# The order of the query blocks in a head pair's attention: 0 to 7, or small and large in turn

## What is computed

```python
SEQ, N_HEADS, HEAD_DIM, N_KV_HEADS = 1024, 8, 64, 2      # 4 query heads per KV head
CMP_BLOCK, CMP_STRIDE, SLC_BLOCK, TOP_K, WINDOW, Q_BLOCK = 32, 16, 64, 16, 512, 128

def nsa_core(q, qpos, gates, cmp_kv, fetch, n_sel, win_kv, win_pos):
    ...
    s = jnp.einsum('btkgd,bnkd->bkgtn', qg, cmp_kv[:, :, 0]) - slopes * d_c.astype(F32)
    p_cmp = masked_softmax(s, d_c >= 0)
    o_cmp = jnp.einsum('bkgtn,bnkd->btkgd', p_cmp, cmp_kv[:, :, 1])
    ...
    _, idx = lax.top_k(score, min(TOP_K, n_sel))
    sel = fetch(idx)
    ...
    p = masked_softmax(s, d_s >= 0)
    o_slc = jnp.einsum('bkgtm,bktmd->bkgtd', p, vsel)
    ...
    mask_w = (d_w >= 0) & (d_w < WINDOW) & (win_pos[None, :] >= 0)
    p = masked_softmax(s, mask_w)
    o_win = jnp.einsum('bkgts,bskd->btkgd', p, win_kv[:, :, 1].astype(F32))
    o = g[:, :, 0] * o_cmp + g[:, :, 1] * o_slc + g[:, :, 2] * o_win
```

## Time and profile before

| | us |
|---|---|
| median of 3 runs | 1961.72 (1958.79 to 1964.0) |
| the profiled execution | 1964.53 |
| its span | 1962.7 |
| mean granted TensorE clock | 0.974 |

### The profile page before, as it was taken

One profiled execution on the slowest core, in us unless ns is written; L12 is line 12 of the kernel. 1 busy time (PEld: TensorE's weight loads), 2 busy tenths in 40 slices (PEclk: granted clock), 3 DMA queues, 4 the chain that ended last, 5 costly groups with the idle time before them and its releaser, 6 DMA issues.

```text
span 1962.7 us, 35065 instructions
## 1 busy us (share of the span) xinstructions
PE 1869.0 (95%) x13394; PEld 1744.7 (89%) x13394; DVE 913.8 (47%) x1621; ACT 658.5 (34%) x1229; POOL 599.1 (31%) x611
## 2 busy tenths in 40 slices
PE   7999989998996989999999999999999999999998
PEld 6999979988994666666799999999999999999898
DVE  5699945665446666767533221212121212224434
ACT  4312222344334666566522321211111121214335
POOL 0003872322304433334353222222222222225531
PEclk8999987999998999999999999999999999999998
DMA  5322364533513344333313112111111111112113
GB/s 156 90 77 52 76 184 112 158 91 101 159 45 108 101 122 125 116 118 114 111 54 127 43 33 59 33 55 38 49 39 53 43 44 54 38 44 92 54 33 132
DMA packets 192571, 163.66 MB, mean 83 GB/s; under 512 B 23092, under 2 KB 175361, under 8 KB 191759
## 3 DMA queue, kind: packets, MB, share of 16 engines
q1 hardware_dynamic: 174781, 137.01, 23.7%
q0 software_dynamic: 6336, 17.31, 3.3%
q10 hardware_dynamic: 11290, 7.09, 1.3%
HBM read 147.70 MB, written 18.25 MB: 85 GB/s over the span
## 4 chain that ended last, share of the span: by engine, by line
PE 32%; issue 23%; POOL 8%; DVE 3%; ACT 2%; POOLq 0%; DVEq 0%; ACTq 0%
PE ps L206 10%; POOL wm_lo L192 6%; PE ps L2168 5%; PE ps L2540 4%; PE ps L1610 3%; PE ps L1622 3%; PE ps L1599 3%; PE ps L1649 2%; DVE S L1868 1%; PE ps L2557 1%; ACT S L1749 1%; PE ps L1657 1%; PE ps L1685 1%; POOL S L1566 1%; PE ps L2577 0%
## 5 line engine op out<-in xcount | busy, mean ns | idle before, releaser
L192 POOL TENSOR_TENSOR wm_lo<-wm_raw,wm_hi 128x512 fp32r<-128x512 f32 (+1 forms) x96 | 169.1, 1762 | 556.8 <-ACT wm_hi L187 556.8
L2357 DVE TENSOR_TENSOR xT<-ps,xT 128x1056 f32<-128x1056 f32 x64 | 80.5, 1258 | 259.9 <-PE ps L206 259.9
L1566 POOL TENSOR_SCALAR S<-S,inv,gate_p 128x64 f32<-128x64 f32 (+6 forms) x192 | 123.2, 662 | 207.2 <-DVE inv L1878 207.2
L206 PE MATMUL ps<-Ahi,wm_hi 128*128 128x352 f32 x768 | 167.5, 326 | 4.4 <-POOL wm_lo L192 2.5
L187 ACT ACTIVATE wm_hi<-wm_raw 128x512 fp32r<-128x512 f32 (+1 forms) x96 | 73.9, 769 | 286.4 <-PE ps L206 286.4
L206 PE MATMUL ps<-Hhi,wm_hi 128*128 128x352 f32 x768 | 167.1, 326 | 1.3 <-POOL wm_lo L192 1.3
L902 PE MATMUL ps_p<-Xhi,w1hi 128*128 128x256 f32 (+1 forms) x544 | 164.4, 302 | 2.9 <-DVE Xlo L1087 2.9
L206 PE MATMUL ps<-Alo,wm_hi 128*128 128x352 f32 x768 | 166.0, 324 | 0.0
L206 PE MATMUL ps<-Ahi,wm_lo 128*128 128x352 f32 x768 | 166.0, 323 | 0.0
L206 PE MATMUL ps<-Hhi,wm_lo 128*128 128x352 f32 x768 | 165.6, 323 | 0.0
L206 PE MATMUL ps<-Hlo,wm_hi 128*128 128x352 f32 x768 | 165.3, 323 | 0.0
(11 more groups left out here) (383 smaller groups left out, 3999.0 us busy)
## 6 DMA issues: line engine op xcount, KB each, us to landing
s_raw<-in_cache_slc_kv_dram SPq DMA_DIRECT2D x256, 128.0 KB, 2.1
raw<-in_cache_cmp_kv_dram SPq DMA_DIRECT2D x128, 128.0 KB, 4.2
raw<-in_cache_cmp_kv_dram POOLq DMA_DIRECT2D x128, 128.0 KB, 4.4
wm_raw<-in_w_up_dram SPq DMA_DIRECT2D x32, 512.0 KB, 4.0
wm_raw<-in_w_down_dram SPq DMA_DIRECT2D x64, 256.0 KB, 2.7
win_raw<-in_w_in_dram SPq DMA_DIRECT2D x38, 256.0 KB, 3.4
wg_raw<-in_w_ple_gate_dram SPq DMA_DIRECT2D x14, 512.0 KB, 3.9
xT<-x_spill SPq DMA_DIRECT2D x2, 2112.0 KB, 10.8
```

What stands on the lines that cost most here:

```text
L192: self.c.nc.gpsimd.tensor_tensor(self.lo[s][:, 0:nk, :], self.raw[s % self.raw_slots][:, 0:nk, :], self.hi[s][:, 0:nk, :].bitcast(F32), AL ...
L206: mm = nc.tensor.matmul(ps[:, j, 0:CH], w[s][:, k, :], x(k)[:, CH * j:CH * j + CH], start=(k == 0 and n == 0), stop=(k == nk - 1 and n == 2))
L1566: nc.gpsimd.tensor_scalar(x, x, inv[:, n % 3, 3 * e + br:3 * e + br + 1], c.gate_p[:, i, H * br + h:H * br + h + 1], ALU.mult, ALU.mult).t ...
L2357: nc.vector.tensor_tensor(three(x), banks[s][:, :, 0:CH], three(x), ALU.add).then_inc(W.free, 1)
```

## The change

Two tables are changed. The blocks of a head pair are taken in the order 0, 7, 1, 6, 2, 5, 3, 4, and the tiles of scores have other places, such that three neighbours of the new order don't overlap. What follows from the order changes with it: the units scored ahead of the first step are blocks 0 and 7; block 0 hosts 1, block 7 hosts 6, 1 hosts 2, 6 hosts 5, 2 hosts 3, 5 hosts 4, 3 hosts the next pair's 0, and 4 its 7; the last units are blocks 3 and 4.

```diff
-S_PLACE = {7: 0, 6: 6912, 5: 13312, 4: 0, 3: 5376, 1: 9728, 0: 13312, 2: 14592}
+BLOCK_ORDER = (0, 7, 1, 6, 2, 5, 3, 4)
+S_PLACE = {7: 0, 6: 6912, 5: 13312, 4: 7680, 3: 3328, 1: 14336, 0: 13056, 2: 0}
...
-    UNITS = [(g, i) for g in range(G) for i in range(QB)]
+    UNITS = [(g, i) for g in range(G) for i in BLOCK_ORDER]
```

## The result

The changed kernel takes 1972.87 us in the median of 5 runs (1970.81 to 1974.06), against 1961.72 (1958.79 to 1964.0): a ratio of 1.0054, 95% interval 1.0044 to 1.0065. It is slower, by 11 us. 1976 was forecast.

The account below looks back on a forecast made before the run. The attention stage was taken to last TensorE's own work plus its idle time. Terms 10.2 + 2.3 - 2.9 + 2.65 + 1.5 = 13.75 us over 1961.7 gave 1976 us; own range 1969 to 1984, 8 in 10 within 1960 to 1988.

Parts of the forecast that it names:

- part 1: Block 0 before block 7, three places: 6.26 us chain against 2.88 us of TensorE work; idle 8.9 us in sum.
- part 3: Decoding quads' exps on ScalarE: TensorE's waits for them grow from 5.9 to 8.2 us, +2.3 us.
- part 4: ScalarE's copy of finished output blocks: TensorE's waits for it fall from 10.3 to 7.4 us, -2.9 us.
- smaller waits: TensorE's other idle time, with the end of the stage some 9 us; no change entered in the sum.
- part 5: Start of the attention stage, blocks 0 and 7 scored ahead: +4.5 us, less 1.85 of work already done, +2.65 us.
- part 6: TensorE's clock falls behind two of the three long waits, the old fall gone or moved: +1.5 us, bounds 0 and 3.
- Part 2: Blocks 1, 2 and 3 before 6, 5 and 4: waits for scaled scores of 3.3, 2.6 and 0.6 us.
- three long waits: TensorE's waits of part 1: 3.4 us at steps 44 and 66, 2.1 us at step 22.
- rival (a): No difference within 0.3%: the waits don't add up and the constants hide the start; 5 us, 1967; chance 0.19.
- Rival (b): Faster: large blocks' light steps are filled, 17 us won against 12.9 of new waits and start; 1957; chance 0.15.
- Rival (c): Slower by more: the clock falls after every wait over 1.2 us, some ten times, +15 us; 1989; chance 0.08.

Follow-up runs that it names:

- e1: The changed kernel again, unedited: 1975.72 us, ratio 1.0061.
- e2: The changed kernel, with ScalarE doing block 7's late exps before keeping the transposed bank in block 0's one step: 1967.33 us, ratio 1.0023.
- e5: The old order, with ScalarE copying the finished output before keeping the transposed bank in step 1 of a unit: 1954.29 us, ratio 0.9951.
- e4: The changed kernel, with the first head pair in the old order and score tiles placed unit by unit: 1972.16 us, ratio 1.0057.
- e7: The changed kernel with the ScalarE list edits of e2, e5 and e6: 1951.73 us, ratio 0.9938.
- e6: The old order with e5's edit, and ScalarE doing a quad's exps before the late exps of the hosted block: 1950.60 us, ratio 0.9939.
- e3: The changed kernel, with 24 extra TensorE transposes in the wait before block 7 in the third and fourth pair: 1970.17 us, ratio 1.0046.

## Why the prediction was right, point by point

The time is 3 us under the forecast in the first measurement and at the forecast in e1 (1975.72); the sign and the places of the long waits are right. That the sum comes out to 0.1 us for the stage is luck: the clock was put 7.4 us too low, and the other terms together as much too high, the waits for scaled scores alone by 3.1.

| term of the sum | predicted us | in the profile after |
|---|---|---|
| part 1, block 0 before 7 (in the next row too) | 8.9 | 3.35 + 3.35 + 2.1 = 8.8 |
| parts 1 and 2, all waits for scaled scores | 15.4 (+10.2) | 10.4, and 12.3 with the 1.9 us for VectorE's queue (+7.1) |
| part 3, quads' exps | 8.2 (+2.3) | 8.2 (+2.3) |
| part 4, output copy | 7.4 (-2.9) | 5.9 (-4.4) |
| smaller waits | 0 | -1.9, without the 1.9 counted above |
| part 5, start, net of work done ahead | +2.65 | 4.04 - 2.35 = +1.7 |
| part 6, clock | +1.5 | 331.8 - (325.2 - 2.35) = +8.9 |
| the stage | +13.75 | +13.7 |

- Part 1 holds to 0.1 us, link by link: the step above is the chain that was worked out. In the second pair the last link was another one than named. VectorE's queue behind the blocked reciprocal held the bank for the quad's scores, and TensorE waited 1.9 us for that and 0.2 for GpSimd. The prediction has that queue in it, but said that it lies inside the same 6.3 us, which it does. e2 shows that the place of the late exps is the cause of 1.4 of the 3.35 us in the third pair and of 2.2 in the fourth.
- Part 2 was too high. Block 1 before 6 gave 1.6, 0, 1.1 and 0.1 us for 1.7, 0, 1.3 and 0.3, but block 2 before 5 gave 0, 0, 0.4 and 0.4 for 2.6 in all, and block 3 before 4 nothing for 0.6. There other waits of the same step (a kept bank of keys 0.6, the quads' exps) came first and covered it. That is rival (a)'s mechanism at work in the small.
- Part 3's sum is right, and so are its places: quads 1, 4, 5, 6, 11 and 13. The single waits are off by up to 0.2 us.
- Part 4's sign and cause hold; its size was under-estimated by 1.5 us. e5 says how to read it: most of the old order's waits were due to the copy's place behind the keep.
- Part 5: the first transposes come 14.85 us into the stage instead of 10.81, 4.0 us later where 4.7 were expected. The 2.35 us of work done ahead are an estimate, block 7's scores less block 1's at the prices of the prediction. The prediction itself measured at a later point, the first transposes of the second block, where it had 4.5 - 1.85 = 2.65:

```profile
615.54 1.09 PE L1611 MATMUL ps<-ident,S 128*128 128x128 f32 x8
```

  That is 23.96 us into the stage, against 18.84 for 613.70 in the old order: 5.1 us later, 3.3 net. The difference to the table's 1.7 is counted there in part 6 and in the smaller waits. e4 gives 2.7 to 3.2 us for the start and the rest of the first pair together.
- Part 6 is the step that failed in size. Four falls were there instead of the two foreseen: behind the waits that end at 654.5 (1.24 us), 799.8 (3.35; this fall is twice as long as the others), 874.7 (0.95 and 1.72, in steps 61 and 62) and 897.1 (3.35). They hold the lower level for 17 us where the old kernel's one fall held it for 3.4; at half rate that is 6.8 us more. The other 2 us of the table's 8.9 are the stretch of lower level that began in the longer start and ran on to 615.0. I had let two of the three long waits bring falls, which is what happened, and took the short ones for harmless, which they are not always: two falls stand behind 1.24 + 0.27 and 0.95 + 1.72 us, while 1.29 + 0.58 (at 710) and 1.30 + 0.70 (at 817) in the old kernel brought none. The timed runs agree in kind: their mean granted clock is 0.975 before the change, and 0.973 and 0.972 in the two measurements of the changed kernel, 4 to 7 us of lost time. The sentence on the Trainium skill's rule (TensorE: Matmul & The Clock Gate, Part 1) gave 1977 for three falls behind the three long waits: the trace agrees with the direction, but the wait of the second pair brought no fall, and shorter ones did.
- In time of the whole kernel the stage's 13.7 us showed up as 11.2, and as 14.0 in e1. The stages behind took 999.6 and 998.1 us in the two profiles of the new order, 1000.5 and 999.8 in those of the old; that is no more than they move in other kernels.
- Rival (a) as a whole falls by the time: its 1967 lies under every run of the changed kernel.
- Rival (b), balance, has the wrong sign, and e5 to e7 show why. With ScalarE's list mended, the old order (1950.6) and the new one (1951.7) are the same within the noise, with 21.8 and 22.0 us of TensorE's idle time. So balance was not what held up the old order. Rival (c) is true in part: falls behind waits as short as 1.24 us exist, but two, not ten.
- Two signs were too high: GpSimd's wait total is 14.4 us where 18 was foretold, and the last product comes at 972.6 where 976 was, 3.3 us of it because the stage began earlier.

e6 and e7 beat both kernels, by 0.61% and 0.62% against the kernel before; no interval reaches 1.

## What to carry to other kernels

When an order of work is permuted, look at the shortest unit first and ask what must be finished while it runs: here a unit of 2.9 us had to cover a chain of 6.3. Before balancing the load, look where in each engine's list the waited-for instruction stands; two swaps in ScalarE's list gave 11 to 12 us in the old order, while the permutation cost 11, and with the list mended made no difference in time. Idle time of TensorE in a sum needs two entries, the wait and the slower work behind it, and the second has a wide range: waits under 2 us were followed by a fall in some places and not in others.

## What was not expected of the hardware

- A wait of 3.35 us was followed by 6.8 us of the lower clock level in the third pair, in both profiles of the changed kernel, but by 3.4 us in the fourth pair, and in e4 by 3.4 us in both. From the end of the wait on TensorE was busy throughout.
- The old kernel's one mid-stage fall came in both profiles behind 629 us, the new order's four came again at the same places, one of them twice as long, with two more (730.4 and 965.9). The waits repeat to 0.1 us, the falls behind them less: the wait of 1.41 us in the second pair had a fall behind it in e1, e2 and e3, and none in the first profile and in e4.
- The time around the stage moves by more than the clock of the stage explains: its start lay between 591.0 and 595.2 us, and what follows it took 994.7 to 1000.5, in kernels whose other stages are the same instruction for instruction. Most of it is the clock of these stages: with half of their time at the lower level taken off, which is an estimate, the part ahead comes to 561.8 to 563.7 us and the part behind to 989.9 to 993.7. One profile is good for a stage, not for the total.
